# A decoder layer in float32: the delta rule's outputs and the last phase with tokens on partitions

## The reference

```
proj = rms_norm(x, norm_mix) @ w_in             # u, v, q, k, v, z, beta, a, gates
o = gated_delta_rule(q, k, v, g, beta)          # 16 heads of 128, chunked, with a carried state
o = rms_norm(o, dn_out_norm) * silu(z)          # per token and head, over 128 features
merged = gate_a * (y_a @ w_branch_a) + gate_b * (y_b @ w_branch_b)
x = x + merged @ w_out
x = x + (silu(f_gate) * f_up) @ w_down
ple_gate = sigmoid(rms_norm(x, ple_norm) @ w_ple_gate)
x = x + ple_gate * (p @ w_ple_proj)
return rms_norm(x, norm_final)
```

## Time and profile before

| | |
|---|---|
| runs of the kernel before, us | 1880.5, 2019.01, 1875.2 (median 1880.5) |
| profiled execution, us | 1874.99 |
| its span, us | 1873.3 |
| mean granted clock | 0.991 |
| TensorE matmul busy | 1821.2 us (97%) |
| VectorE busy | 1199.2 us (64%) |
| ScalarE busy | 894.5 us (48%) |
| GpSimd busy | 258.4 us (14%) |
| DMA, mean | 176 GB/s |

### The profile page before, as it was taken

How to read it: one execution, slowest core, us unless ns; L and a number is a source line. 1 busy time by engine, 2 the same in 40 slices (tenths; PEclk the granted TensorE clock), 3 DMA queues, 4 the chain that set the end, 5 groups by cost and what they waited for, 6 DMA issues and landing times.

```text
span 1873.3 us, 30201 instructions
## 1 busy us (share of the span) xinstructions
PE 1821.2 (97%) x10810; PEld 1595.0 (85%) x10810; DVE 1199.2 (64%) x1408; ACT 894.5 (48%) x1030; POOL 258.4 (14%) x374
## 2 busy tenths in 40 slices
PE   7889999999999999999999999999999999999996
PEld 5778888888878888888888888888888888888885
DVE  5776767867646665665677655556555555545676
ACT  5554444545446554545445544444444443444453
POOL 4051240612410000000011000000000000000034
PEclk9989999999999999999999999999999999999998
DMA  6345454453545555565555555555555556565552
GB/s 224 125 140 173 130 172 135 160 185 115 184 155 168 180 181 196 184 196 185 192 189 189 172 194 191 191 185 179 192 192 191 186 175 206 175 199 180 189 178 103
DMA packets 103709, 329.52 MB, mean 176 GB/s; under 512 B 23168, under 2 KB 23312, under 8 KB 103632
## 3 DMA queue, kind: packets, MB, share of 16 engines
q1 hardware_dynamic: 89024, 321.43, 52.3%
q10 hardware_dynamic: 13808, 4.21, 1.0%
q0 software_dynamic: 800, 2.88, 0.4%
HBM read 325.33 MB, written 3.16 MB: 175 GB/s over the span
## 4 chain that ended last, share of the span: by engine, by line
PE 90%; DVE 4%; ACT 2%; issue 2%; DMA 1%; POOL 1%; DVEq 0%; ACTq 0%; SPq 0%; POOLq 0%
PE acc L282 54%; PE acc L287 28%; DVE wlo L275 1%; PE ps L612 1%; PE ps L618 1%; PE acc L303 1%; PE acc L304 1%; PE acc L305 1%; POOL sqsum L457 1%; DMA inv_out<-blk_xT 1%; ACT whi L267 0%; PE ps L665 0%; PE ps L578 0%; ACT ax L962 0%; DVE pre L1323 0%
## 5 line engine op out<-in xcount | busy, mean ns | idle before, releaser
L275 DVE TENSOR_TENSOR wlo<-raw,whi 128x1024 fp32r<-128x1024 f32 x604 | 755.1, 1269 | 436.6 <-ACT whi L267 428.0
L282 PE MATMUL acc<-ax,whi 128*128 128x512 f32 x3328 | 845.4, 396 | 9.8 <-ACT whi L267 9.8
L267 ACT ACTIVATE whi<-raw 128x1024 fp32r<-128x1024 f32 x604 | 624.4, 1054 | 467.5 <-PE acc L287 435.1
L282 PEld LDWEIGHTS acc<-ax,whi 128*128 128x128 f32 x3328 | 602.3, 190 | 121.4 <-issue 12.0
L287 PEld LDWEIGHTS acc<-ax,wlo 128*128 128x128 f32 x3328 | 455.3, 191 | 33.1 <-DVE wlo L275 0.2
L287 PE MATMUL acc<-ax,wlo 128*128 128x256 f32 x3328 | 465.0, 283 | 0.0
L282 PE MATMUL acc<-fx,whi 128*128 128x512 f32 x704 | 176.3, 392 | 0.0
L282 PEld LDWEIGHTS acc<-fx,whi 128*128 128x128 f32 x704 | 126.6, 189 | 22.6
L521 POOL TENSOR_TENSOR sqsum<-sqsum,t 128x512 f32<-128x512 f32 x16 | 22.1, 1378 | 706.5 <-ACT t L1222 706.5
L927 ACT ACTIVATE t<-acc 128x512 f32<-128x512 f32 x88 | 52.4, 596 | 131.6 <-PE acc L287 131.6
L1323 DVE TENSOR_TENSOR t<-acc,t 128x512 f32<-128x512 f32 x88 | 60.7, 690 | 81.1 <-ACT t L927 80.7
(11 more groups left out here) (244 smaller groups left out, 1338.9 us busy)
## 6 DMA issues: line engine op xcount, KB each, us to landing
raw<-in_win SPq DMA_DIRECT2D x224, 512.0 KB, 3.5
raw<-in_wgu SPq DMA_DIRECT2D x176, 512.0 KB, 4.4
raw<-in_wd SPq DMA_DIRECT2D x88, 512.0 KB, 4.2
raw<-in_wb SPq DMA_DIRECT2D x32, 512.0 KB, 4.5
raw<-in_wo SPq DMA_DIRECT2D x32, 512.0 KB, 4.5
raw<-in_wpg SPq DMA_DIRECT2D x32, 512.0 KB, 3.6
raw<-in_wa SPq DMA_DIRECT2D x16, 512.0 KB, 4.9
xT<-in_xT SPq DMA_DIRECT2D x4, 512.0 KB, 6.7
```

What stands on the lines that cost most here:

```text
L267: nc.scalar.activation(whi[:, s], raw[:, s], ACT.Copy).then_inc(hi_done, 1)
L275: nc.vector.tensor_tensor(wlo[:, s], raw[:, s], whi[:, s].bitcast(F32), ALU.subtract).then_inc(lo_done, 1)
L282: nc.tensor.matmul(o, whi[:, s, kt, m * P:(m + 1) * P], x[:, k].rearrange("p q n -> p (q n)"), start=begin, stop=False, skip_group_check=True)
```

## The change

The delta rule's outputs come out with tokens on partitions: in `outputs` the operands of the three products of a head are exchanged. ScalarE copies instead of squaring, GpSimd squares (`square_o`, behind its load of the next group's rows), VectorE sums along the free axis and scales o by the root (`o_inv` in step 14, `o_scale` in step 16), TensorE turns the eight 128x128 blocks back (`turn_o`, step 16), and VectorE applies gain and z on the way out (`norm_o`, step 17). `o_columns`, `o_row`, `o_gain` and `o_diagonal` go; ScalarE's root moves from step 14 to 15.

In the last phase, x is turned so that tokens are on partitions (`turn_x`, 32 transposes in two parts, `copy_x`), and `proj` and `ple` give rows: three units of 512 features, and two of 256 (`narrow`, 24 matmuls of 256 columns a half), the last of which does one token tile after the other. The norms are then values per partition. The final gain is a row spread over all partitions, loaded by GpSimd. Each token tile is scaled by VectorE, ScalarE and GpSimd in parts and stored by SyncE and ScalarE. The output tensor has tokens first.

```diff
 (plan)
-        ("down", 2, 4 * HFF, (2, 2)), ("proj", 1, 4, (2, 2)), ("ple", 2, 4 * HID, (2, 2))]
+        ("down", 2, 4 * HFF, (2, 2)), ("proj", 1, 4, (2, 2)), ("ple", 1, 3 * HWIDE + 2 * HID, (3, 2))]
 (gpsimd)
+            def square_o(d):
+                pool.wait_ge(delta_act, 3 * d + 3)
+                g.tensor_tensor(t[0][:], t[2][:], t[2][:], ALU.mult).then_inc(o_squared, 1)
...
                 load_rows(pool, d + 1, g_in)
+                square_o(d)
...
 (tensor)
-                    mm(psv[1][:, h, 0:P], vnew[:, h], qkT[:, h], start=True, stop=True)
-                    mm(psv[1][:, h, P:SEQ], vnew[:, 4 + h], qkT[:, 4 + h], start=True, stop=False)
-                    last = mm(psv[1][:, h, P:SEQ], state[:, h], qdec[:, h], start=False, stop=True)
+                    mm(psq[1][:, 2 * h], qkT[:, h], vnew[:, h], start=True, stop=True)
+                    mm(psq[1][:, 2 * h + 1], qkT[:, 4 + h], vnew[:, 4 + h], start=True, stop=False)
+                    last = mm(psq[1][:, 2 * h + 1], qdec[:, h], state[:, h], start=False, stop=True)
-            def o_columns(d):
-                pe.wait_ge(delta_act, 3 * d + 3)
...
-            def o_row(d):
-                pe.wait_ge(o_diag, d + 1)
-                rows(t[2], o_rows)
+            def turn_o(d):
+                pe.wait_ge(o_scaled, d + 1)
+                if not isinstance(d, int):
+                    pe.wait_ge(k_normed, d + 2)
+                for x in range(8):
+                    last = nc.tensor.transpose(psq[0][:, x], t[2][:, x // 2, x % 2 * P:(x % 2 + 1) * P], ident[:])
+                last.then_inc(o_turned, 1)
-                      11: second_tile, 12: outputs, 13: o_columns, 14: o_row}
+                      11: second_tile, 12: outputs, 16: turn_o}
...
+            first = {0: ple_sum, 2: lambda: turn_x(0), 5: turn_last}
+            for u in range(3):
+                gemm("ple", 0, u * HWIDE, HWIDE, u % 2, u // 2, ax, rows=True, after=first if u == 0 else None)
...
+            for m in range(TILES):
+                for n in range(HID):
+                    pe.wait_ge(lo_done, half_of("ple", 0, n0 + n) + 1)
+                    last = narrow(n0 + n, HALF_K * n, 0, m, n == 0, n == HID - 1)
+                last.then_inc(ple_tile, 1)
 (scalar)
-            def square_o(d):
+            def copy_o(d):
                 act.wait_ge(delta_out, 5 * d + 5)
-                f(t[2][:], psv[1], ACT.Square).then_inc(delta_act, 1)
+                f(t[2][:], psv[1], ACT.Copy).then_inc(delta_act, 1)
-                      13: (square_o,), 14: (o_rt,)}
+                      13: (copy_o,), 15: (o_rt,)}
...
+            for m in range(TILES):
+                act.wait_ge(ple_tile, m + 1)
+                ple_sigmoid(4, m)
+                f(preload[:, m:m + 1], ones[:, 0:1], ACT.Sqrt)
+                ple_square(4, m)
+                act.wait_ge(fin_inv, 2 * m + 2)
+                f(xroot[:, m:m + 1], xmean[:, m:m + 1], ACT.Sqrt).then_inc(fin_root, 1)
+                act.wait_ge(fin_root, m + 1)
+                act.wait_ge(ple_gain, 2 * len(UNITS) - 2)
+                f(xtok[:, m, OUT_ACT], xtok[:, m, OUT_ACT], ACT.Copy, scale=xroot[:, m:m + 1]).then_inc(out_act, 1)
...
 (vector)
             def o_inv(d):
-                dve.wait_ge(o_len, d + 1)
-                v.scalar_tensor_tensor(length[:, 2], psf[0][:, 16:24], 1.0 / P, length[:, 0], ALU.mult, ALU.add).then_inc(o_mean, 1)
+                dve.wait_ge(o_squared, d + 1)
+                v.tensor_reduce(length[:, 2], t[0][:].rearrange("p h (m n) -> p (h m) n", n=P), mybir.AxisListType.X, ALU.add).then_inc(o_mean, 1)
+                dve.wait_ge(o_mean, 3 * d + 1)
+                v.scalar_tensor_tensor(length[:, 2], length[:, 2], 1.0 / P, length[:, 0], ALU.mult, ALU.add).then_inc(o_mean, 1)
...
+            def o_scale(d):
+                dve.wait_ge(o_root, d + 1)
+                o = t[2][:].rearrange("p h (m n) -> p (h m) n", n=P)
+                v.tensor_tensor(o, o, bc(length[:, 2], P), ALU.mult).then_inc(o_scaled, 1)
+            def norm_o(d):
+                dve.wait_ge(o_turned, d + 1)
+                dve.wait_ge(z_silu, 2 * d + 2)
                 o = oT[:, ds(GROUP * d, GROUP)]
+                v.scalar_tensor_tensor(o, psv[0], cols[:, C_DNO:C_DNO + 1], o, ALU.mult, ALU.mult).then_inc(ps_free, 1)
-                      9: (copy_invT64,), 10: (copy_nwT,), 11: (copy_state,), 13: (o_gain,), 14: (o_inv, o_diagonal), 15: (norm_o,)}
+                      9: (copy_invT64,), 10: (copy_nwT,), 11: (copy_state,), 14: (o_inv,), 16: (o_scale,), 17: (norm_o,)}
```

More of the change, by code:

```diff
@@ L184, in build @@
     praw = t[1][:, 0:PLE // P]
+    sig = [t[n][:].rearrange("p (m a) n -> p m (a n)", m=TILES) for n in (0, 2)]
+    squares = t[1][:].rearrange("p (m a) n -> p m (a n)", m=TILES)
     pre_at = cursor[0]
@@ L408, in _ @@
                 load_half(sp, wpp, n * P, half_of("proj", 0, n), n)
[L409 to L419, removed]
+            for n in range(PER["ple"]):
+                load_half(sp, wpg, n * P, half_of("ple", 0, n), n)
+            for m in range(TILES):
+                sp.wait_ge(out_dve, 2 * m + 1)
+                sp.dma_start(out_rows(m, OUT_DVE), xtok[:, m, OUT_DVE]).then_inc(stored, 16)
+                sp.wait_ge(out_dve, 2 * m + 2)
+                sp.wait_ge(out_pool, m + 1)
+                last = slice(OUT_POOL.start, OUT_LAST.stop)
+                sp.dma_start(out_rows(m, last), xtok[:, m, last]).then_inc(stored, 16)
+            sp.wait_ge(stored, 16 * 3 * TILES)
         @block.gpsimd
@@ L498, in _ @@
             v0 += INV_STEPS
+            square_o(NGROUPS - 1)
             pool.wait_ge(vT_out, NGROUPS)
@@ L530, in _ @@
             residual(1)
[L531 to L554, removed]
+            pool.wait_ge(half_used, H0["proj"])
+            pool.dma_start(gfin[:], fin_d.to_broadcast([P, D])).then_inc(fin_in, 16)
+            chain(g.memset(eye[:], 0.0), v0 + 1)
+            g.affine_select(out=eye[:], in_=eye[:], compare_op=ALU.not_equal, fill=1.0, base=0,
+                            pattern=[[-1, P]], channel_multiplier=1).then_inc(eye_again, 1)
+            pool.wait_ge(fin_in, 16)
+            for u, (c, w) in enumerate(UNITS[:-1]):
+                for m in range(TILES):
+                    pool.wait_ge(ple_sq, 2 * u + m + 1)
+                    x = xtok[:, m, c:c + w]
+                    g.tensor_tensor(x, x, gfin[:, c:c + w], ALU.mult).then_inc(ple_gain, 1)
+            for m in range(TILES):
+                pool.wait_ge(ple_gain, 2 * len(UNITS) - 2)
+                pool.wait_ge(fin_root, m + 1)
+                x = xtok[:, m, OUT_POOL]
+                g.tensor_tensor(x, x, xroot[:, m:m + 1].to_broadcast([P, OUT_POOL.stop - OUT_POOL.start]), ALU.mult).then_inc(out_pool, 1)
         @block.tensor
@@ L906, in _, with turn_last @@
-            for k in range(2):
-                last = mm(psf[0][:, 0:SEQ], ones[:], t[1][:, 2 + k], start=False, stop=(k == 1))
-            last.then_inc(sq_summed, 1)
+                acc_free(pe, "proj", 0, n % 2, n // 2)
+                use_half(pe, "proj", 0, n, n % 2, True, True, 0, px, rows=True)
+            def turn_last():
+                pe.wait_ge(res[1]["lo"], 8)
+                turn_x(1)
+            pe.wait_ge(res[1]["lo"], 6)
+            first = {0: ple_sum, 2: lambda: turn_x(0), 5: turn_last}
@@ new lines, in _ @@
+            for u in range(3):
+                gemm("ple", 0, u * HWIDE, HWIDE, u % 2, u // 2, ax, rows=True, after=first if u == 0 else None)
+            n0 = 3 * HWIDE
+            acc_free(pe, "ple", 0, 1, 1)
+            for n in range(HID):
+                pe.wait_ge(lo_done, half_of("ple", 0, n0 + n) + 1)
+                for m in range(TILES):
+                    last = narrow(n0 + n, HALF_K * n, 1, m, n == 0, n == HID - 1)
+                last.then_inc(half_used, 1)
+            n0 += HID
```

302 lines of the change are left out of this document (150 added, 152 removed).

## The result

The changed kernel takes 1893.3 us (median of four runs, 1891.3 to 1893.9); the kernel before, run beside it, took 1875.2 (median of three runs, 1874.5 to 1880.5; a fourth, of 2019.0 us, fell in the chip's slower state and counts in no comparison). The ratio on record is 1.0090, with a 95% interval of 1.0075 to 1.0104: slower by 0.9%. The forecast was 1893, with a range of 1877 to 1906. The profiled execution took 1893.59 us for a span of 1891.8.

The account below looks back on a forecast made before the run. The prediction took TensorE, near nine tenths busy in every slice, as the bound. It summed 1875.0 + 12.6 (wait) + 7.8 (clock) + 5.0 (last group) - 7.0 (last phase) = 1893.4, forecast 1893 us, range 1877 to 1906.

Parts of the forecast that it names:

- Step 1: TensorE in each group: column sums and row broadcast go, eight transposes come; -2.6 us a group if nothing waited.
- Step 4: TensorE's transposes in step 16 wait 6.8 us for VectorE's scaling of o: +4.2 us a group, +12.6 over three passes.
- Rival A: Delta-rule groups, step 16: VectorE's scaling is there before TensorE asks, so the removal pays as written: 1857.6 us; chance 12%.
- if nothing waited: TensorE's removed work less the new transposes, with no new wait: -2.6 us a group, -10.4 over four.
- Step 2: The square on GpSimd takes 2.8 us (1.4 to 5.5), hidden because VectorE waits for its split anyway: priced at nothing.
- Step 3: VectorE's step 14: the reduction over 1024 elements takes one pass, 1.14 us; the convolution behind comes 0.28 us earlier.
- Step 5: After the loop passes' idle, TensorE's granted clock falls to 0.50: +2.6 us a pass, +7.8 over three.
- Step 6: The last group, inside the wide V blocks: +2.4 us of wait (idle 5 us) and +2.6 of clock, together +5.0.
- Step 7: The last phase: TensorE ends 2.8 us later, the tail behind it shrinks from 18.3 to 8.5 us: -7.0 together.
- Rival D: The last phase's tail gives nothing back, through stores bound by landing or TensorE stalling for splits: 1900 us; chance 5%.
- rival B: TensorE's new wait comes but the clock holds, without the 10.4 us of clock terms: 1883 us; chance 11%.

Follow-up runs that it names:

- experiment 1: The changed kernel with TensorE's `turn_o` in step 18 instead of 16 and VectorE's `norm_o` in 19 instead of 17: 1876.0 us, ratio 0.9995.
- experiment 2: The changed kernel with `turn_o` in step 19 and `norm_o` in 20 in the loop passes, 18 and 19 in the last group: 1878.8 us, ratio 1.0017.
- experiment 3: The changed kernel with VectorE's `o_scale` in step 15, behind make_negm, instead of 16; `turn_o` stays in 16: 1868.7 us, ratio 0.9965.
- experiment 7: On experiment 3's kernel, VectorE's diff_q moved from step 17 to 13 in the loop passes and `o_scale` put ahead of make_negm: 1858.2 us, ratio 0.9899.
- experiment 9: The changed kernel with GpSimd's square done twice, one behind the other: 1892.9 us, ratio 1.0097.
- experiment 4: The changed kernel with useless matmuls filling most of TensorE's idle ahead of `turn_o`, 26 in a loop pass, 18 in the last group: 1883.3 us, ratio 1.0043.
- the half alone: The kernel before with only the last phase changed to tokens on partitions, groups as before: 1867.0 us, ratio 0.9946.
- experiment 8: On experiment 7's kernel, ScalarE issues store_m in step 16 and load_m in 17 instead of 15 and 16: 1857.5 us, ratio 0.9903.

## Why the prediction was right, step by step

**Steps 1 and 4, the removed work and the new wait.** The idle was forecast at 6.8 us in a loop pass and about 5 in the last group; it was 6.90, 7.09, 6.96 and 5.04. Experiments 1 to 3 show it to be a matter of place: with either end moved, these 26 us shrink to 1.7, nothing and 4.5. What the forecast said of the later steps held only while TensorE was the late one: VectorE's two added passes hid behind TensorE's 7 us. Rival A, "the removal pays as written", was put at 1857.6. It did not come, and a small chance was right for this kernel. With VectorE's order mended (experiment 7) the time is 1858.2, near the rival's. That is in part luck, since the rival had no moved steps. In that trace p starts at 1740.15, 11.6 us ahead of the kernel before (the forecast's "if nothing waited" is 10.4), and 1.6 of these are the fall of the clock at 31.83, which this trace does not have:

```profile
1740.15 0.40 PE L321 MATMUL acc<-whi,px 128*128 128x512 f32 x1
```

My expectations of experiments 1, 2 and 3 took such a value as given once the wait was moved, and missed by 18, 22 and 7 us: I had counted TensorE's time and not whether VectorE could keep up with a TensorE that is 2.6 us a group faster, nor that each new wait could bring the clock down again.

**Step 2, the square.** 1.88 us in place of 2.8, within the bounds, and hidden either way (experiment 9). The rule of the Trainium skill (GPSIMD Engine Reference, "Engine selection": about twice VectorE's time for two inputs) gave an estimate of 2.4; the trace says 1.88, 1.5 times VectorE's 1.22 for a multiply of the same size (`o_scale`).

**Step 3, the reduction.** One pass was taken, 1.14 us from start to start; it was 1.24 (452.68 to 453.92).

**Steps 5 and 6, the clock.** Right in place: the granted clock is 0.50 behind each of the four idles, and the two groups of instructions took 1.97 and 3.76 us in the loop passes, as in the earlier trace rows. The size was a little high, because 2.6 was added up from durations. From start to start, the fall costs 2.5 us in a loop pass (1.62, 3.56 and 1.09 us in place of 0.85, 1.93 and 0.95 in experiment 4) and 2.1 in the last group, where the eight matmuls took 3.39: 9.7 us in all for 10.4. Experiment 4 gave 10.0. The groups' 25.8 us against a forecast of 25.4 is thus closer than the terms are.

**Step 7, the last phase.** TensorE ends 2.6 us later in it (forecast 2.8), and the tail is 8.4 us against 18.3 (forecast 8.5). By the runs the half alone is worth 10.2 us of the medians, by the traces 7.2 to 7.5; the profiled execution of before (1875.0) lies under its median in that batch (1877.2), which is most of the difference. Rival D is out by this, and rival B by the 0.50 rows and by experiment 4.

**The best version** of these runs is experiment 7 or 8, which can't be told apart: 1.0% faster than the kernel before and 1.9% faster than the changed one. It keeps every instruction of the change and moves two of VectorE's steps.

## What to carry to other kernels

When TensorE gives work away to engines that run beside it, find for each result that it still needs from them the step at which that engine delivers it in its own order, with the queues of its feeders, and place TensorE's step by that. Here the same instructions cost 0.9% or gained 1.0%, by where two of VectorE's steps stand. An idle of TensorE is paid twice where it brings the clock down; and when it is removed, ask which engine is late next before counting the gain.

## What the runs showed of the hardware that was not expected

- GpSimd's square of a 128x1024 tile with itself took 1.88 us, less than two of the 128x512 operations on two tiles (1.38 each on average).
- VectorE and GpSimd slow each other when both run wide operations. In the last phase of the kernel before, GpSimd's sum of squares took 1.28 us while VectorE was idle and 2.27 beside VectorE's splits. In the last phase of the changed kernel, two splits of 1.2 us took 4.56 us while GpSimd's two gain multiplies took 3.74. In the delta-rule stretch, next to GpSimd's small operations, the same split went only from 1.22 to 1.35.

```profile
1837.83 2.27 POOL L537 TENSOR_TENSOR sqsum<-sqsum,t 128x512 f32<-128x512 f32 x1
...
1852.70 1.28 POOL L537 TENSOR_TENSOR sqsum<-sqsum,t 128x512 f32<-128x512 f32 x1
```

```profile
1868.27 4.56 DVE L293 TENSOR_TENSOR wlo<-raw,whi 128x1024 fp32r<-128x1024 f32 x2
```

```profile
1868.01 3.74 POOL L568 TENSOR_TENSOR xtok<-xtok,gfin 128x512 f32<-128x512 f32 x2 [18.19 <-ACT t L1308]
```

- The length of an idle does not settle by itself whether TensorE's clock falls. The work behind it ran at the 1.2 GHz level after the idles of 3.15 to 7.13 us in these experiments, and at full clock after those of 1.8 us and less. In between both were seen: in experiment 3 the clock fell behind 2.79 and 2.65 us and held behind 2.67 at the same place, and behind the wait of 2.24 us for the inversion it fell in the changed kernel and held in experiments 4 and 7. A fall cost from 1.4 us (behind 7.13 us of idle, in the kernel with the groups alone changed) to 3.3 (behind 3.16, in experiment 2) in the two groups of instructions behind it, so a longer idle did not cost more.
- Executions of one kernel differ by such falls. The eight of experiment 3 run from 1865.5 us at a mean granted clock of 0.994 to 1874.3 at 0.989; only one of them has rows, so which idles made the difference is not shown. A change of two or three microseconds should be read from its rows, with such falls set aside.
